# A two-block transformer kernel: the calls of the first attention, of the gated delta rule and of the start of the last attention in another order

## The chip, the cores and the metric

The kernel runs on one core of one Trainium2 chip. The metric is the device time of one launch in microseconds (us); the median over runs is compared. The five engines are called PE (TensorE, matmuls), DVE (VectorE), ACT (ScalarE), POOL (GpSimd) and SP (SyncE, which issues the DMAs).

## The reference, cut to what matters

256 tokens of width 1024 go through two blocks. The first has two layers, each an attention and an MLP; the second has a gated delta rule layer (GDN) and a last attention (FoX) on shared keys and values.

```python
def mla_mixer(h, ...):                       # first attention, 8 heads
    proj = h @ w_in                          # 384 q rank, 256 kv rank, 64 rope
    q  = (rms_norm(c_q,  g) @ w_uq)          # 8 x (128 nope + 64 rope)
    kv = (rms_norm(c_kv, g) @ w_ukv)         # 8 x (128 k + 128 v)
    q_pe = rope(rms_norm(q_pe, g), cos, sin)
    ...                                      # softmax(q k^T + q_pe k_pe^T) v, then w_o

def gdn_mixer(h, ...):
    qkv, z, a, b = split(h @ w_in)
    qkv = silu(causal_depthwise_conv(qkv, conv_w))
    ...                                      # g = log decay, beta
    a_mat = where(strict, (k*beta) @ k^T * decay, 0)    # 64 x 64, a chunk and a head
    sol = triangular_solve(a_mat, [v*beta, k*beta*exp(gcum)], unit_diagonal=True)
    ...                                      # 4 chunks in turn
    o = rms_norm_2(o, o_norm) * silu(z)
    return o @ w_out

def second_block(x, ...):
    h = x + rms_norm_2(gdn_mixer(...), g)
    k, v, c = shared_kv(h, ...)              # c: cumulated forget gate
    return h + rms_norm_2(fox_mixer(h, k, v, c, ...), g)
```

## The kernel before

Every engine has a program of its own inside `bass_two_blocks`: `tensor_program`, `scalar_program`, `vector_program`, `gpsimd_program`, `sync_program`. Each first defines small functions (one step each) and then calls them in a list **written out by hand**. An engine works its list strictly in order. Steps wait for each other by semaphores inside the functions, so the list sets what stands in front of what, and nothing else does. Nearly all instructions are recorded by a helper, so the profile shows one line each: PE's matmuls are L491 and its transposes L499, ACT's L1376 (table loads L1379), DVE's L2309, L2312 and L2315, POOL's L3525.

**Weights** come in 136 chunks through `RING` = 3 raw buffers: chunks 0 to 13 belong to the first attention (0 to 3 its first projection; kv, uq, uq, kv, uq, uq are 4 to 9; 10 to 13 the output weights), 14 to 45 to its MLP, 94 to 114 to GDN (109 and 110 the last of z, 111 to 114 the output weights), 115 to 135 to the last attention. float32 is split in two: `hi(c)` on ACT writes the high part `whi`, then `lo(c)` on DVE the rest `wlo` = `raw` - `whi`. For the chunks 104, 106, ..., 114 (`ON_POOL`) POOL does `lo(c)`, in four instructions. `hi(c)` waits until PE has finished chunk c-3. On PE a chunk is four quarters; `to(n, q)` works off the quarters up to, not including, quarter q of chunk n. A uq chunk issues something only in its quarters 1 and 3. Activations are split alike (`xhl`, in the last part of the inverse used again; `oth` and `otl`).

**First attention.** `turn_x` transposes the input, chunks 0 to 3 give the projection in four PSUM banks; `proj_scale` (half on ACT, half on DVE) reads them, `turn_c(0..4)` transposes the result, chunks 4 to 9 follow. `bias_mm` builds the relative bias of the second attention from indicator rows that DVE makes (`bias_ind`, 1.22 us each). For each of four head pairs i POOL rotates q (`q_rope(i)`: one multiplication and 12 small instructions, all on POOL), `qp_T(i)` transposes what it made, then `score_pair`, softmax on DVE and ACT (`logits`, `exp`, `over_sum`, `divide`), `turn_p`, `value`.

**GDN.** `sums(h)`, `rw_T`, `row_bc(h)`, `kq(h)` and DVE's `block_(h)` build for each of 8 heads the triangular matrix. The inverse is made for four groups of two heads, g = 0..3, in two pairs. `inv_0`, `inv_c`, `inv_r` and DVE's `inv_d`, `inv_b` (13 small dependent instructions), `inv_e` make the 8 x 8 diagonal blocks. Then come the levels l = 3..6: PE's `inv_w(g,l)` (product), ACT's copy, PE's `inv_x(g,l)` (product), DVE's addition, PE's `inv_v(g,l)` (transpose), ACT's copy; POOL masks one operand of each level. Then `inv_f`, `inv_t`, `inv_y` and `sol(h, part)`, the solution. `conv_pre`, `conv_taps`, `conv_acc` and `v_silu` are the convolutions and their silu, `v_T` turns v, `z_silu(pair, t)` is the silu of z. Groups 0 and 1 run at 696 to 717 us, groups 2 and 3 from 719 us on.

**Start of the last attention.** `turn_xf` transposes the sum of the residual; `xhi_kv` and `xlo_kv` split it; chunk 116 on needs them.

Of the kernel before, what the change touches and what calls it, by code (L numbers as in the profile page):

```python
# [132 lines left out]
def bass_two_blocks(nc, A, out):  # L133

    ctx = ExitStack()
    with ctx:
# [335 lines left out]
        def tensor_program(eng):  # L472
# [35 lines left out]
            def quarter(c, q):  # L508
# [3 lines left out]
                if q == 0:  # L512
                    L.wait_ge(*LO[c])
# [636 lines left out]
            to(104, 3)  # L1150
            sums(5)
            to(105, 3)
            sums(6)
            to(106, 1)
            sums(7)
            to(106, 3)
            rw_T()
            to(107, 0)
            row_bc(0)
            row_bc(1)  # L1160
            kq(0)
            to(107, 1)
            row_bc(2)
            to(107, 2)
            row_bc(3)
            kq(1)
            to(108, 1)
            kq(2)
            row_bc(4)
            to(108, 2)  # L1170
            kq(3)
            row_bc(5)
            to(109, 0)
            kq(4)
            kq(5)
            to(109, 1)
            row_bc(6)
            row_bc(7)
            kq(6)
            to(109, 2)  # L1180
            kq(7)
            inv_c(0)
# [18 lines left out]
            inv_x(1, 4)  # L1201
            inv_x(0, 4)
# [2701 lines left out]
```

## Time and profile before

| | us |
|---|---|
| median of 3 runs (lowest, highest) | 922.52 (921.96, 923.47) |
| span of the profiled execution | 920.4 |
| PE busy | 892.8 (97%) |
| DVE, ACT, POOL busy | 623.8, 525.5, 78.3 |
| DMA, mean rate | 155 GB/s |

The profile is of one execution. PE is busy nearly all the time and makes up 88% of the chain that ended last, so read it by PE's gaps: in which stretch PE is not busy, and what it waits for there.

### The profile page before, as it was taken

Reading aid. Unit: us, or ns where it says so; the run is one execution under the profiler, and the core shown is the slowest. Engines: PE = TensorE matmul, PEld = TensorE weight load, DVE = VectorE, ACT = ScalarE, POOL = GpSimd, SP = SyncE. Lnnn points to the kernel's source line nnn. Section 1 sums busy time; section 2 is a strip of 40 time slices with the busy share of each in tenths; the row PEclk is TensorE's granted clock in tenths of the full one; section 3 lists DMA queues with packets and bytes.
Section 4 is the critical chain, followed back from the end, with each engine's and each line's share of the span. In section 5 each row is a group of like instructions: output and inputs, shape, how many; then the busy total and the mean of one; then the engine's idle time right before and its main releaser. Section 6 shows DMA issues by size and latency. Waiting matters only on the chain.

```text
span 920.4 us, 13095 instructions
## 1 busy us (share of the span) xinstructions
PE 892.8 (97%) x5254; PEld 774.4 (84%) x5254; DVE 623.8 (68%) x1033; ACT 525.5 (57%) x848; POOL 78.3 (9%) x96
## 2 busy tenths in 40 slices
PE   6899999999999999999999999999999999999997
PEld 6777888888888888888888888999988888798885
DVE  6887686756666576657655556696786666776775
ACT  5788644435444686636444434565546565657782
POOL 0055000000000000000000000002535312000000
PEclk9999999999999999999999999999999799999999
DMA  8442456535554544447555654555430041654411
GB/s 261 138 150 81 138 183 245 187 137 184 201 195 153 183 137 141 150 153 242 179 189 175 222 197 139 182 160 166 138 101 37 5 157 46 203 190 180 165 65 46
DMA packets 61677, 142.67 MB, mean 155 GB/s; under 512 B 5296, under 2 KB 7344, under 8 KB 61616
## 3 DMA queue, kind: packets, MB, share of 16 engines
q1 hardware_dynamic: 61616, 141.83, 45.3%
q8 instruction: 42, 0.69, 0.3%
q14 instruction: 19, 0.16, 0.1%
HBM read 140.77 MB, written 1.05 MB: 154 GB/s over the span
## 4 chain that ended last, share of the span: by engine, by line
PE 88%; DVE 4%; POOL 3%; issue 2%; ACT 1%; SPq 1%; DMA 0%; DVEq 0%; POOLq 0%; ACTq 0%
PE ps L491 85%; PE ps L499 4%; POOL arena L3525 3%; SPq L3617 1%; DVE wlo L2309 1%; DVE sub L2309 1%; ACT arena L1376 0%; ACT whi L1376 0%; DVE xhl L2309 0%; POOL otl L3525 0%; DMA pint<-rel_bias_table_dram 0%; DVE arena L2309 0%; DVE X L2309 0%; DVE arena L2315 0%; ACT otl L1376 0%
## 5 line engine op out<-in xcount | busy, mean ns | idle before, releaser
L2309 DVE TENSOR_TENSOR wlo<-raw,whi 128x2048 fp32r<-128x2048 f32 (+3 forms) x130 | 286.8, 2214 | 121.7 <-ACT whi L1376 121.5
L1376 ACT ACTIVATE whi<-raw 128x2048 fp32r<-128x2048 f32 (+3 forms) x136 | 250.8, 1852 | 178.7 <-PE ps L491 166.7
L491 PE MATMUL ps<-xhl,whi 128*128 128x512 f32 (+3 forms) x928 | 257.7, 348 | 0.0
L491 PE MATMUL ps<-xhl,wlo 128*128 128x256 f32 x720 | 202.5, 281 | 0.0
L491 PEld LDWEIGHTS ps<-xhl,whi 128*128 128x128 f32 (+2 forms) x928 | 158.9, 186 | 25.0
L491 PE MATMUL ps<-whi,xhl 128*128 128x512 f32 (+2 forms) x528 | 168.9, 388 | 1.9 <-DVE xhl L2315 1.7
L491 PE MATMUL ps<-whi,oth 128*128 128x512 f32 x416 | 164.8, 396 | 0.2 <-DVE otl L2315 0.2
L491 PE MATMUL ps<-whi,otl 128*128 128x512 f32 x416 | 162.4, 390 | 0.0
L491 PE MATMUL ps<-wlo,oth 128*128 128x512 f32 x416 | 162.1, 390 | 0.0
L491 PEld LDWEIGHTS ps<-xhl,wlo 128*128 128x128 f32 x720 | 134.9, 187 | 0.8
L491 PEld LDWEIGHTS ps<-whi,xhl 128*128 128x128 f32 x528 | 99.2, 190 | 18.9 <-DVE wlo L2309 3.2
L491 PE MATMUL ps<-wlo,xhl 128*128 128x512 f32 (+2 forms) x264 | 100.1, 379 | 0.0
L1376 ACT ACTIVATE arena<-ps 128x256 f32<-128x256 f32 (+3 forms) x136 | 51.5, 417 | 77.2 <-PE ps L491 68.8
L491 PEld LDWEIGHTS ps<-whi,otl 128*128 128x128 f32 x416 | 78.1, 188 | 16.8
L491 PEld LDWEIGHTS ps<-whi,oth 128*128 128x128 f32 x416 | 78.1, 188 | 16.3 <-issue 0.7
L491 PEld LDWEIGHTS ps<-wlo,oth 128*128 128x128 f32 x416 | 78.2, 188 | 15.0
L3525 POOL TENSOR_TENSOR wlo<-raw,whi 128x512 fp32r<-128x512 f32 x24 | 35.0, 1488 | 600.4 <-ACT whi L1376 600.4
L2309 DVE TENSOR_TENSOR arena<-ps,arena 128x256 f32<-128x256 f32 (+2 forms) x104 | 45.7, 470 | 40.5 <-ACT arena L1376 20.3
L491 PE MATMUL ps<-arena 128*128 128x128 f32 (+3 forms) x384 | 65.9, 324 | 0.3
L1376 ACT ACTIVATE arena<-ps,st 128x512 f32<-128x512 f32 (+3 forms) x66 | 40.5, 639 | 41.0 <-PE ps L491 16.0
L491 PEld LDWEIGHTS ps<-arena 128*128 128x128 f32 (+1 forms) x384 | 55.7, 195 | 6.8 <-issue 1.7
L491 PEld LDWEIGHTS ps<-wlo,xhl 128*128 128x128 f32 x264 | 50.3, 191 | 7.1
(146 smaller groups left out, 880.9 us busy)
## 6 DMA issues: line engine op xcount, KB each, us to landing
raw<-mlp_w_in_dram SPq DMA_DIRECT2D x32, 1024.0 KB, 5.2
raw<-mlp_w_out_dram SPq DMA_DIRECT2D x32, 1024.0 KB, 5.0
raw<-gdn_w_in_dram SPq DMA_DIRECT2D x16, 1024.0 KB, 5.3
raw<-moba_w_qkv_dram SPq DMA_DIRECT2D x12, 1024.0 KB, 5.2
raw<-kv_w_dram SPq DMA_DIRECT2D x8, 1024.0 KB, 5.4
raw<-fox_w_in_dram SPq DMA_DIRECT2D x8, 1024.0 KB, 5.2
raw<-mla_w_o_dram SPq DMA_DIRECT2D x4, 1024.0 KB, 5.4
raw<-moba_w_o_dram SPq DMA_DIRECT2D x4, 1024.0 KB, 5.9
```

Source lines behind the costliest of these rows:

```text
L491: return eng.matmul(o, l, r, start=start, stop=True, skip_group_check=True)
L499: return eng.transpose(o, i, ident)
L1376: return eng.activation(o, i, f, **kw)
L2309: return eng.tensor_tensor(o, a, b, f)
L3525: return eng.tensor_tensor(o, a, b, f)
L3617: eng.dma_start(o, i).then_inc(s_in, 16)
```

## The change

The change gives the lists of PE, ACT and DVE the same calls as before, in another order, in three regions; POOL's and SP's lists stay word for word. Nothing of the computation changes. One condition is new: a uq chunk waits for its `lo` in quarter 1 and not in quarter 0, which issues nothing.

Cut to its core (`...` is left out; in GDN, `kq`, `row_bc` and `sums` move ahead of several quarters in the same manner):

```diff
-                if q == 0:
+                if q == (1 if kind == "uq" else 0):
                     L.wait_ge(*LO[c])
...
# tensor_program, first attention
+            to(0, 2)
             turn_x("mla", 3)
-            to(1, 3)
+            to(4, 0)
             bias_mm(0)
-            to(4, 0)
             turn_c(0)
...
             score_pair(0)
-            to(8, 2)
+            to(9, 2)
             qp_T(1)
-            to(9, 2)
             turn_p("mla", 0)
+            turn_p("mla", 1)
             score_pair(1)
-            turn_p("mla", 1)
...
-            to(10, 3)
+            to(11, 0)
             q_T(2)
             qp_T(2)
-            to(11, 0)
+            q_T(3)
             turn_p("mla", 2)
-            q_T(3)
+            turn_p("mla", 3)
             score_pair(2)
-            turn_p("mla", 3)
             qp_T(3)
...
# tensor_program, GDN
             to(109, 0)
-            kq(4)
-            kq(5)
+            inv_0(0)
             to(109, 1)
...
-            to(109, 3)
-            inv_r(0)
-            to(110, 1)
-            v_T(0, 0)
-            inv_0(0)
-            v_T(0, 1)
             inv_0(1)
             inv_w(0, 3)
-            v_T(1, 0)
+            kq(7)
             inv_w(1, 3)
+            to(109, 2)
+            v_T(0, 0)
             inv_x(0, 3)
             inv_x(1, 3)
-            v_T(1, 1)
-            inv_v(0, 3)
+            to(109, 3)
             inv_v(1, 3)
             inv_w(1, 4)
+            inv_v(0, 3)
             inv_w(0, 4)
+            to(110, 1)
+            inv_x(0, 4)
+            inv_x(1, 4)
             to(110, 2)
...
             inv_y(0)
-            inv_t(1)
             inv_r(1)
             sol(0, 0)
+            inv_t(1)
...
             inv_x(3, 5)
-            to(111, 1)
             inv_x(2, 6)
             inv_v(3, 5)
             inv_w(3, 6)
+            to(111, 1)
+            inv_x(3, 6)
...
# scalar_program, first attention
             rsq("mla_x")
-            hi(4)
+            proj_scale()
             hi(5)
-            hi(6)
-            proj_scale()
...
# scalar_program, GDN
             ln_sums()
+            conv_acc(8)
+            hi(106)
+            hi(107)
...
             inv_w(1, 3)
+            hi(111)
+            inv_y(1, 3)
             inv_y(0, 3)
-            z_silu(0, 0)
-            inv_y(1, 3)
+            inv_w(0, 4)
+            conv_acc(11)
             inv_w(1, 4)
-            z_silu(0, 1)
-            inv_w(0, 4)
-            z_silu(1, 0)
+            hi(112)
+            v_silu(1)
             inv_y(1, 4)
...
             inv_t(0)
-            hi(113)
+            z_silu(1, 0)
             z_silu(1, 1)
+            inv_t(1)
+            sol(0, 0)
             table("natural_log_exp_and_others")
-            inv_t(1)
...
             sol(2, 0)
+            hi(113)
# vector_program, first attention
             bias_table()
-            bias_ind(0)
             lo(2)
...
# vector_program, GDN
             inv_x(0, 3)
             inv_x(1, 3)
-            v_beta(1, 1)
-            lo(111)
+            conv_taps(10)
+            conv_taps(11)
             inv_x(1, 4)
             inv_x(0, 4)
...
# tensor_program, start of the last attention
             turn_xf(0, 1)
-            to(115, 0)
+            to(114, 3)
             turn_xf(0, 2)
```

**ACT at the projection's scaling**, before. `arena<-ps,st 128x352` are `proj_scale`'s two halves, `whi<-raw` a chunk's `hi` (here 4, 5 and 6):

```order
19 L1376 ACTIVATE st<-st 128x2 [waits s_rm]
20 L1376 ACTIVATE st<-st 128x2 [waits o_act]
21 L1376 ACTIVATE whi<-raw 128x2048 [waits s_w,s_raw1]
22 L1376 ACTIVATE whi<-raw 128x1152 [waits s_w,s_raw2]
23 L1376 ACTIVATE whi<-raw 128x1152 [waits s_w,s_raw0]
24 L1376 ACTIVATE arena<-ps,st 128x352 [waits s_rs]
25 L1376 ACTIVATE arena<-ps,st 128x352
```

The same place of the change:

```order
20 L1372 ACTIVATE st<-st 128x2 [waits s_rm]
21 L1372 ACTIVATE st<-st 128x2 [waits o_act]
22 L1372 ACTIVATE arena<-ps,st 128x352 [waits s_w,s_rs]
23 L1372 ACTIVATE arena<-ps,st 128x352
24 L1372 ACTIVATE whi<-raw 128x1152 [waits s_raw2]
25 L1372 ACTIVATE xhl<-ps,cols 128x256 [waits s_pt_] x3
```

The scaling now stands ahead of `hi(5)` and `hi(6)`; `hi(4)` went further ahead.

**PE in level 3 of groups 0 and 1**, before. `ps<-cst` are transposes, `oth,otl` and `otl,oth` the level's products (`inv_w`, `inv_x`), `ps<-cst,arena` here `v_T`:

```order
3114 L491 MATMUL ps<-oth,otl 128x128 [waits g_v,g_il0,g_ia0]
3115 L491 MATMUL ps<-oth,otl 128x128 x3
3116 L499 MATMUL ps<-cst,arena 128x128 [waits g_sv]
3117 L499 MATMUL ps<-cst,arena 128x128 x3
3118 L491 MATMUL ps<-oth,otl 128x128 [waits g_v,g_il1,g_ia1]
3119 L491 MATMUL ps<-oth,otl 128x128 x3
3120 L491 MATMUL ps<-otl,oth 128x128 [waits g_ia0]
3121 L491 MATMUL ps<-otl,oth 128x128 x3
3122 L491 MATMUL ps<-otl,oth 128x128 [waits g_ia1]
3123 L491 MATMUL ps<-otl,oth 128x128 x3
```

The same place of the change; `whi,xhl` and `wlo,xhl 128x512` are a quarter of chunk 109, `ps<-arena` are `kq(7)`:

```order
3091 L491 MATMUL ps<-oth,otl 128x128 [waits g_il1,g_ia1]
3092 L491 MATMUL ps<-oth,otl 128x128 x3
3093 L491 MATMUL ps<-whi,xhl 128x512
3094 L491 MATMUL ps<-wlo,xhl 128x512
3095 L491 MATMUL ps<-whi,xhl 128x512 x2
3096 L491 MATMUL ps<-wlo,xhl 128x512
3097 L491 MATMUL ps<-whi,xhl 128x512
3098 L499 MATMUL ps<-cst,arena 128x128 [waits g_ia0,g_sv]
3099 L499 MATMUL ps<-cst,arena 128x128 x3
3100 L491 MATMUL ps<-otl,oth 128x128 [waits g_ba]
3101 L491 MATMUL ps<-otl,oth 128x128 x3
```

A quarter now stands between `inv_w(1,3)` and `inv_x(0,3)`, whose input ACT copies meanwhile.

**ACT where pair 1 begins**, before. `oth<-ps` with g_ip0 is `inv_t(0)`, with g_ip1 `inv_t(1)`; `whi<-raw` is `hi(113)`:

```order
508 L1376 ACTIVATE oth<-ps 128x512 [waits g_ip0]
509 L1376 ACTIVATE whi<-raw 128x2048 [waits s_w,s_raw2]
510 L1376 ACTIVATE arena<-ps,st 128x512
511 L1379 ACT_TABLE_LOAD
512 L1376 ACTIVATE oth<-ps 128x512 [waits g_ip1]
```

The same place of the change:

```order
507 L1372 ACTIVATE oth<-ps 128x512 [waits g_ip0]
508 L1372 ACTIVATE arena<-ps,st 128x512 [waits s_w] x2
509 L1372 ACTIVATE oth<-ps 128x512 [waits g_ip1]
510 L1372 ACTIVATE arena<-ps 128x128 [waits g_sp0]
511 L1375 ACT_TABLE_LOAD
```

`inv_t(1)` no longer stands behind `hi(113)` and the table load, but behind two `z_silu`.

## Rows read from the trace of the kernel before

**Rows 1.** The page: busy time of the engines, and the chain by engine
```profile
PE 892.8 (97%) x5254; PEld 774.4 (84%) x5254; DVE 623.8 (68%) x1033; ACT 525.5 (57%) x848; POOL 78.3 (9%) x96
PE 88%; DVE 4%; POOL 3%; issue 2%; ACT 1%; SPq 1%; DMA 0%; DVEq 0%; POOLq 0%; ACTq 0%
```
**Rows 2.** Windows: length, busy us (count) of each engine, granted clock, DMA share, GB/s
```profile
600.00:630.00 30.00, 30.00 (x252) 30.00 (x253) 28.05 (x49) 18.13 (x25) 0.00 (x0) 1.00 0.54 176
690.00:700.00 10.00, 9.41 (x63) 8.22 (x62) 7.33 (x24) 7.81 (x9) 2.37 (x3) 1.00 0.24 93
700.00:710.00 10.00, 9.12 (x67) 7.95 (x67) 6.55 (x9) 6.44 (x12) 7.85 (x7) 1.00 0.00 0
720.00:730.00 10.00, 8.13 (x37) 7.41 (x38) 5.19 (x18) 5.05 (x10) 2.50 (x3) 0.61 0.00 0
730.00:740.00 10.00, 9.93 (x78) 9.72 (x78) 6.50 (x14) 6.50 (x17) 3.68 (x4) 0.88 0.46 157
```
**Rows 3.** PE's waits at 0 to 112 us: total, times, longest
```profile
PE ps L499 <- DMA X<-x_dram: 7.7, 1, 7.7
PE ps L499 <- POOL arena L3525: 3.4, 4, 1.5
PE ps L499 <- ACT arena L1376: 2.2, 1, 2.2
```
**Rows 4.** Timeline, 28 to 33 us: start, duration, engine, instruction, [idle before <-releaser]
```profile
28.69 1.16 ACT L1376 ACTIVATE whi<-raw 128x1152 fp32r<-128x1152 f32 x1 [1.30 <-PE ps L491]
28.71 1.08 DVE L2312 TENSOR_SCALAR arena<-ps,st 128x352 f32<-128x352 f32 x2 [1.79 <-PE ps L491]
29.76 0.98 ACT L1376 ACTIVATE arena<-ps,st 128x352 f32<-128x352 f32 x2
30.80 1.10 PE L499 MATMUL ps<-cst,arena 128*128 128x128 f32 x8 [2.20 <-ACT arena L1376]
32.92 0.76 PE L491 MATMUL ps<-whi,xhl 128*128 128x512 f32 x1 [1.03 <-DVE xhl L2315]
```
**Rows 5.** Timelines of PE and POOL, 60 to 85 us: q's rotation and who waits
```profile
60.48 0.33 PE L491 MATMUL ps<-wlo,xhl 128*128 128x384 f32 x1
60.65 0.34 PE L491 MATMUL ps<-whi,xhl 128*128 128x384 f32 x1
62.33 0.44 PE L499 MATMUL ps<-cst,arena 128*128 128x128 f32 x2 [1.34 <-POOL arena L3525]
72.06 0.99 POOL L3525 TENSOR_TENSOR arena<-arena,st 128x256 f32<-128x256 f32 x1 [9.79 <-DVE st L2315]
84.52 0.44 PE L499 MATMUL ps<-cst,arena 128*128 128x128 f32 x2 [1.52 <-POOL arena L3525]
```
**Rows 6.** POOL's timeline: `lo` of chunks 104 and 110
```profile
631.13 5.04 POOL L3525 TENSOR_TENSOR wlo<-raw,whi 128x512 fp32r<-128x512 f32 x4 [546.67 <-ACT whi L1376]
681.00 7.08 POOL L3525 TENSOR_TENSOR wlo<-raw,whi 128x512 fp32r<-128x512 f32 x4 [14.00 <-ACT whi L1376]
```
**Rows 7.** PE's waits at 690 to 750 us, and one of 750 to 810
```profile
PE ps L491 <- ACT oth L1376: 1.4, 1, 1.4
PE ps L499 <- DVE oth L2309: 0.6, 1, 0.6
PE ps L491 <- ACT otl L1376: 0.5, 2, 0.3
...
PE ps L491 <- DVE xhl L2315: 0.7, 1, 0.7
```
**Rows 8.** Timeline, 717 to 724 us: start of pair 1
```profile
717.41 1.91 ACT L1376 ACTIVATE whi<-raw 128x2048 fp32r<-128x2048 f32 x1
719.91 1.28 ACT L1379 ACT_TABLE_LOAD   x1
722.95 1.29 DVE L2309 TENSOR_TENSOR xhl<-sub,blk 128x512 fp32r<-128x512 f32 x2
723.70 1.97 PE L499 MATMUL ps<-cst,xhl 128*128 128x128 f32 x8 [0.51 <-DVE xhl L2309]
```

More of the change, by code:

```diff
@@ L1154, in tensor_program @@
+            to(105, 0)
+            rw_T()
+            to(105, 1)
+            row_bc(0)
+            to(105, 2)
+            row_bc(1)
             to(106, 1)
-            sums(7)
+            kq(0)
+            kq(1)
+            row_bc(2)
+            row_bc(3)
             to(106, 3)
[L1157 to L1166, printed above, removed]
+            kq(2)
@@ L1167, in tensor_program @@
+            kq(3)
+            row_bc(4)
+            row_bc(5)
+            to(108, 0)
+            kq(4)
             to(108, 1)
-            kq(2)
-            row_bc(4)
+            row_bc(6)
+            inv_c(0)
+            kq(5)
+            row_bc(7)
             to(108, 2)
-            kq(3)
-            row_bc(5)
+            inv_r(0)
+            kq(6)
             to(109, 0)
-            kq(4)
-            kq(5)
+            inv_0(0)
             to(109, 1)
-            row_bc(6)
-            row_bc(7)
@@ L1197, in tensor_program @@
             inv_v(1, 3)
             inv_w(1, 4)
+            inv_v(0, 3)
             inv_w(0, 4)
+            to(110, 1)
+            inv_x(0, 4)
+            inv_x(1, 4)
             to(110, 2)
-            inv_x(1, 4)
-            inv_x(0, 4)
+            v_T(0, 1)
             inv_v(1, 4)
             inv_w(1, 5)
+            v_T(1, 0)
             inv_v(0, 4)
+            v_T(1, 1)
             inv_w(0, 5)
@@ L2131, in scalar_program @@
             inv_w(0, 5)
+            z_silu(0, 1)
             inv_y(1, 5)
@@ L2136, in scalar_program @@
             inv_t(0)
-            hi(113)
+            z_silu(1, 0)
             z_silu(1, 1)
+            inv_t(1)
+            sol(0, 0)
             table("natural_log_exp_and_others")
-            inv_t(1)
+            inv_0(3)
             sol(1, 0)
-            sol(0, 0)
-            inv_0(3)
             inv_0(2)
@@ L2148, in scalar_program @@
             sol(2, 0)
+            hi(113)
+            sol(0, 2)
             sol(1, 2)
@@ L2948, in vector_program @@
             xlo("mla", 1)
-            gain("mla")
             xlo("mla", 2)
+            lo(1)
             xlo("mla", 3)
-            lo(1)
             read_positions()
             bias_table()
-            bias_ind(0)
             lo(2)
-            mean_x("mla")
             rope_angle()
             lo(3)
-            bias_ind(1)
+            mean_x("mla")
+            bias_ind(0)
+            lo(4)
+            rsq_b("mla_x")
             rope_cos()
-            rsq_b("mla_x")
+            proj_scale()
             rope_table()
-            proj_scale()
-            lo(4)
             c_lo(0)
+            gain("mla")
             c_lo(1)
+            lo(5)
             c_lo(2)
-            bias_add(0)
-            lo(5)
+            lo(6)
+            c_lo(3)
             c_mean()
-            c_lo(3)
             c_lo(4)
             rsq_b("mla_c")
+            k_rope()
+            bias_add(0)
+            bias_ind(1)
             bias_ind(2)
-            k_rope()
-            lo(6)
             k_sums(0)
@@ L2995, in vector_program @@
             over_sum("mla", 0)
+            over_sum("mla", 1)
             k_sums(1)
-            over_sum("mla", 1)
             lo(10)
+            q_sums(2)
+            logits("mla", 2)
             rsq_b("mla_k1")
-            logits("mla", 2)
-            q_sums(2)
             o_lo("mla", 0)
@@ L3315, in vector_program @@
             decay_arg(3)
-            conv_taps(11)
+            conv_pre(9)
+            conv_pre(10)
+            inv_0(0)
             block_(2)
+            block_(3)
             decay_arg(4)
-            inv_0(0)
-            block_(3)
+            inv_0(1)
+            conv_taps(9)
+            conv_pre(11)
             decay_arg(5)
@@ L3323, in vector_program @@
             block_(4)
+            decay_arg(6)
+            inv_d(0)
             block_(5)
-            decay_arg(6)
             decay_arg(7)
-            inv_0(1)
-            block_(6)
-            block_(7)
-            inv_d(0)
             inv_b(0)
@@ L3363, in vector_program @@
             inv_x(2, 3)
+            sol(2)
             lo(113)
-            sol(2)
             inv_x(2, 4)
@@ L3368, in vector_program @@
             inv_x(3, 4)
+            gain("fox")
             rsq_b("gdn_o0")
@@ L3385, in vector_program @@
             out_lo(1)
+            sol(6)
             sol(4)
             sol(7)
-            sol(6)
             sol(5)
@@ L3402, in vector_program @@
             post_add("gdn", 0, 0)
-            gain("fox")
             gained("gdn", 1)
             gained("gdn", 2)
+            post_add("gdn", 0, 1)
             xlo_kv(0, 0)
             xlo_kv(0, 1)
-            post_add("gdn", 0, 1)
             lo(116)
```

282 lines of the change are left out of this document (134 added, 148 removed).

## The prediction

> **What bounds the kernel now.** First the page's busy times and its chain: PE is busy for 892.8 of 920.4 us and makes up 88% of the chain [rows 1]. So a change of order can win only in PE's gaps, 27.6 us in all. Second, the busy time by windows, to see where the gaps lie. Between the regions of the change PE leaves nothing (30.00 of 30.00 us at 600 to 630) [rows 2]; gaps stand at the start, in the first attention, and from 690 to 750 us. Third, PE's waits in those regions. In the first attention 7.7 us are the load of the input before anything can run, and stay. What an order can touch is 3.4 us in four waits for POOL and 2.2 us in one wait for ACT [rows 3]. In GDN it is one wait of 1.4 us for ACT, 0.6 and 0.5 us, and some of 0.2 to 0.3 [rows 7]; the windows 690 to 710 leave 0.59 + 0.88 = 1.47 us of PE idle [rows 2]. Fourth, the clock: the granted clock is 0.61 and 0.88 in the windows 720 to 730 and 730 to 740 [rows 2], so PE ran at 1.2 instead of 2.4 GHz for 2 x (0.39 + 0.12) x 10 = 10.2 us there.
>
> A wait costs more than its bracket says, because the busy time of a matmul overlaps the next one. The last two matmuls before the wait at 62.33 start at 60.48 and 60.65, 0.17 us apart; the next starts 1.68 us later, where the bracket says 1.34 [rows 5]. So each wait counts its bracket and about 0.17 us more.
>
> **First attention, the projection.** Before, chunk 3 is done at about 28.6, then ACT does a `hi` of 1.16 us (28.69) and only then its half of the scaling, 29.76 to 30.74; DVE's half runs 28.71 to 29.79, and the transposes of `turn_c` start at 30.80 [rows 4]. In the change ACT scales first, and its half reads the two banks that are done first, so DVE's half is last: `turn_c` could start at 29.85, which is 0.95 us earlier. On top, `bias_mm(0)` and the `bias_ind(0)` that it waits for no longer stand ahead of chunk 2 and of `lo(2)`. The matmuls of `bias_mm(0)`, 0.6 us, move into the gap before `turn_c`, where PE is idle. I take 0.75 us for that; its bounds are 0 (if `lo(2)` ends as late as before) and 1.2 us (the matmuls and the 0.6 us that PE waits before them). Sum 1.7 us at `turn_c`. The wait of 1.03 us for `c_lo` at 32.92 [rows 4] stays, since ACT and DVE still split what PE has just transposed; I take 1.5 us at chunk 4.
>
> **First attention, the rotations.** POOL's rotations are released by DVE, and PE meets four waits for it, the longest 1.52 us at 84.52 and 1.34 us at 62.33 [rows 3, 5]. The gain at chunk 4 and an earlier `rsq_b` on DVE carry to the first of them: I take 2.1 us, and `qp_T(0)` comes 2.1 us earlier with its wait about as before, because the rotation sets it. `qp_T(1)` was one unit of a uq chunk after `score_pair(0)` and is now three after. A unit is nine matmuls at 0.17 us, 1.6 us [rows 5]; two more are 3.1 us, and the wait of 1.34 is less: it goes, 1.5 us. What is late next is DVE: `turn_p(0)` and `turn_p(1)` come in a row, for 0.3 to 0.4 us. The third rotation sat idle 9.79 us until DVE released it at 72.06, and the wait at 84.52 is for the fourth [rows 5]. The two run back to back, 12.4 us together, so PE's arrival is limited by DVE's release at 72.06, not by PE: PE comes 3.3 us earlier but leaves `qp_T(3)` only as much earlier as the release moves. `q_sums(2)` and `rsq_b("mla_q2")` follow the earlier uq chunks and stand before one `logits` as before: about 2.5 us. So of the gains so far 2.5 us leave the stretch, and PE waits about 2.5 us more than now for POOL. After it, `turn_p(4)` and `turn_p(5)` follow `score_pair(3)` with no quarter between, and cost about 0.5 us. **Attention: 2.0 us, bounds 0.5 and 3.3** (nothing of the release's move; all of it and no new waits).
>
> **GDN, pair 0.** The changed PE list puts a quarter (six matmuls of 512 columns; by the 0.17 us of 384 columns [rows 5], 1.4 us) between `inv_w` and `inv_x` of level 3, and quarters or `v_T` into level 4, where before a level's steps followed each other directly. The waits there are 0.6 (DVE), 0.5 in two (ACT), 0.2 (POOL) and two of 0.2 [rows 7]: with 0.17 each some 2.5 us, and a quarter covers any of them. These quarters are not new work, they are taken from ahead of the inverse. So 2.5 us is the upper bound of this term. Against it stand new tight places. (1) `hi(106)` now comes after `ln_sums` on ACT, and POOL needs 5.04 to 7.08 us for a `lo` [rows 6]: chunk 106 may be late by 0 to 1.1 us. (2) `row_bc(4)`, `lo(108)` and `inv_0(0)` come sooner after what they need from DVE and POOL, 0.1 to 0.5 us each. (3) POOL's mask for level 3 stands behind `lo(110)`, which took 7.08 us where DVE was at work beside it: 0 to 0.8 us. (4) `conv_taps(10)`, `conv_taps(11)` on DVE and `conv_acc(11)`, `hi(112)` (1.9 us, as `hi(113)` in [rows 8]) and `v_silu(1)` on ACT now stand inside the levels, ahead of steps that PE waits for; levels 4 and 5 have quarters only in part: 0.5 to 0.85 us. I take 0.1 + 0.3 + 0.2 + 0.5 = 1.1 us. **Net 1.4 us, bounds 0 and 2.5.** The move of the uq wait costs and gives nothing here, since in GDN there is no uq chunk; in the attention it lets PE pass into chunks that issue nothing, 0 to 0.3 us, counted above.
>
> The Trainium skill ("GPSIMD Engine Reference", Specifications) says that GpSimd shares its SBUF interfaces with VectorE and contends with VectorE instructions of two SBUF inputs. The trace agrees in direction: four instructions took 5.04 us at 631 and 7.08 us at 681 [rows 6]. That speaks against this change, which moves `conv_taps` and `lo(109)` about; it changes only the odds of places (1) and (3).
>
> **GDN, pair 1.** Before, `inv_t(1)` on ACT stands behind `hi(113)` (717.41, 1.91 us), one `z_silu` and a table load (719.91, 1.28 us), and PE waits 1.4 us for it [rows 7, 8]. Now only two `z_silu` of 0.7 us stand ahead. ACT is free 2.5 us sooner. But the next thing PE needs is `inv_0(3)`, which waits for DVE's `inv_d`, `inv_b`, `inv_e`; the last of it starts at 722.95 and PE goes on at 723.70 [rows 8]. DVE's chain there begins with the same inputs and has the same 16 instructions, one after the other. So the wait mostly moves from ACT to DVE and is not removed: 0.3 us, bounds 0 and 1.5. The clock falls at 722 in this very gap [rows 2], and since about 1.5 us of waiting stays in it, I leave the 10.2 us at half rate as they are. One `to(111, 1)` moves between `inv_w(3,6)` and `inv_x(3,6)` and the other quarters between `sol` steps: 0.1 us, bounds -0.3 and 0.4. `sol(0,0)` ahead of the table load on ACT: nothing, it is covered by the DVE chain.
>
> **Start of the last attention.** `turn_xf(0, 2)` comes two quarters earlier and `few_T`, `across`, `c_mm` later. The one wait here, 0.7 us for DVE's `xlo_kv` before chunk 116 [rows 7], hangs on `hi(116)`, `post_square` and `lo(116)` in a row, none of which moves ahead. DVE's `lo(119)` and `lo(120)` ahead of `xlo("fox")` have quarters of chunks 117 and 118 as cover. 0 us, bounds -0.3 and 0.3.
>
> **Sum.** 2.0 + 1.4 + 0.3 + 0.1 + 0 = 3.8 us; since small waits turn up where several steps become tight together, I take 3.5 us. The profiled span is 920.4 and the median 922.52, 2.1 us more outside it. 920.4 - 3.5 + 2.1 = 919.0 us.
>
> **Rivals.** (a) *The clock stays up.* If the gap at 719 to 724 becomes short enough, or later, that the clock doesn't fall, PE gets back up to half of the 10.2 us, less what waits take anyway: 4.5 us more, 914.5 us. For it: the wait for ACT goes. Against it: DVE's chain remains. The attention's short fall of the clock (the 512-column matmul at 32.92 took 0.76 us [rows 4]) is worth at most 1.7 us, and lies in the bounds above. The Trainium skill ("TensorE: Matmul & The Clock Gate", Part 4) says that transposes don't count as PE being busy in the same way. By that rule the levels, a third of them transposes, would draw the clock down as soon as quarters no longer separate them; in the window 700 to 710 they are mixed and the clock is 1.00 [rows 2], so the trace doesn't bear it out, and the change mixes more.
> (b) *The waits form again.* ACT's and DVE's own chains through the levels, and POOL, bound them, whatever PE does between: then the change doesn't do in GDN what it says, the 1.4 us are 0, and the attention gives its lower half, 1.0. 920.4 - 1.0 + 2.1 = 921.5 us. For it: PE was 97% busy, and ACT was not idle (7.81 and 6.44 of 10) [rows 2].
> (c) *Slower.* `hi(111)`, `hi(112)` and `v_silu(1)` on ACT, 4.5 us with 0.7 for the silu, stand in levels 3 to 5 ahead of copies that PE needs. If PE has then less than their length of other work left, it waits 1.9 us or more in one piece, as at 720, and the clock falls there as it fell at 722: another 10 us at half rate, 4.5 us. -3.5 + 1.9 + 4.5 = 2.9 us: 925.4 us. It decides from a gap of about 1.9 us in the levels; before, the longest there is 0.6 [rows 7].
>
> **Chances.** The forecast's case (917 to 920.7): 0.58. Rival (a): 0.12. Rival (b): 0.20. Rival (c): 0.10. The bounds of the terms are 0.5 + 0 + 0 - 0.3 - 0.3 = about 0 and 3.3 + 2.5 + 1.5 + 0.4 + 0.3 = 8.0 us; they will not all lie at one end. The range 914.6 to 922.8 takes in (a) and (b) and leaves out (c) and the tail. A measurement of this kernel can tell about 0.2%, 1.85 us, from no change: faster means below 920.7, slower above 924.4. That gives 0.70 faster, 0.20 the same, 0.10 slower.
>
> **What the profile would show.** Attention right: `turn_c` starts at 29 to 30, the wait before the second rotation's `qp_T` is gone, the one before the fourth is longer but ends near 82. GDN right: the window 690 to 710 leaves under 0.5 us of PE idle, and `inv_0(3)` starts about 3.4 us earlier than 723.70, its releaser still DVE. The clock at 0.5 for about 10 us after it. Wrong: a wait of over 1 us of PE for POOL at chunk 106 or level 3, or for ACT in levels 4 and 5; a clock under 1 before 715; or a gap at `turn_c` as long as before, which would say that DVE, not ACT, had set it.

## The result: 22 us slower, and the profile after

The changed kernel takes 944.62 us (median of 4 runs, 941.39 to 945.32), the kernel before beside it 922.44. The ratio is 1.0238, 95% interval 1.0222 to 1.0253. The forecast was 919.0 us with a range up to 922.8: wrong in sign and far outside.

The page of the changed kernel: span, then busy time (share) and count by engine, then the chain that ended last. These answer to [rows 1].

```profile
span 939.6 us, 13097 instructions
PE 903.0 (96%) x5254; PEld 782.3 (83%) x5254; DVE 640.6 (68%) x1033; ACT 524.8 (56%) x848; POOL 77.3 (8%) x96
PE 83%; DVE 8%; POOL 3%; ACT 2%; issue 2%; SPq 1%; DMA 0%; DVEq 0%; ACTq 0%; POOLq 0%
```

Read three things from it. PE is idle for 939.6 - 903.0 = 36.6 us, before 27.6: 9.0 us more of waiting. PE is busy for 10.2 us more with the same 5254 matmuls: they took longer. And DVE is busy for 16.8 us more with the same 1033 instructions, which no part of the prediction had allowed for. Waiting and longer matmuls together are the 19.2 us between the two spans. The profiled run is the quickest of the four (941.39); its mean granted clock is 0.981, that of the others 0.972 to 0.974, before 0.991.

Windows of the changed kernel, columns as in [rows 2]: length, busy us (count) of PE, PEld, DVE, ACT, POOL, then the granted clock, DMA share and GB/s.

```profile
640.00:650.00 10.00, 7.67 (x56) 7.43 (x54) 7.54 (x19) 4.91 (x9) 0.00 (x0) 0.86 0.05 8
650.00:660.00 10.00, 10.00 (x58) 9.89 (x58) 2.25 (x12) 5.48 (x6) 4.68 (x4) 0.63 0.28 100
690.00:700.00 10.00, 6.31 (x30) 5.08 (x29) 9.02 (x18) 4.53 (x7) 7.22 (x6) 0.92 0.30 106
700.00:710.00 10.00, 10.00 (x63) 8.75 (x61) 4.48 (x11) 4.49 (x6) 2.29 (x2) 0.91 0.01 3
730.00:740.00 10.00, 8.88 (x44) 7.47 (x44) 6.33 (x20) 4.57 (x10) 2.46 (x3) 0.66 0.00 1
750.00:760.00 10.00, 8.41 (x40) 7.72 (x41) 8.00 (x21) 4.94 (x11) 1.31 (x1) 0.66 0.76 289
780.00:790.00 10.00, 7.04 (x26) 5.71 (x27) 6.32 (x8) 3.36 (x5) 1.97 (x2) 0.83 0.31 105
```

The stretch around 650, where PE left nothing before, now has a gap and half rate. At half rate PE ran for 2 x (1 - 0.981) x 939.6 = 36 us in all, before for 2 x (1 - 0.991) x 920.4 = 17 us.

PE's waits from 630 to 790 us in the changed kernel, the long ones (total, times, longest); before, those of [rows 7] were 1.4, 0.6, 0.5 and 0.7. The first row is two waits, 3.6 us in front of `out_T(3)` and 1.6 in front of `out_T(0)`; the others stand in front of `inv_0(0)`, `sums(4)`, `inv_c(1)` and `kq(5)`:

```profile
PE ps L499 <- DVE arena L2311: 5.1, 2, 3.6
PE ps L499 <- DVE oth L2305: 3.7, 1, 3.7
PE ps L491 <- DVE st L2308: 2.3, 1, 2.3
PE ps L491 <- DVE xhl L2305: 1.1, 1, 1.1
PE ps L491 <- DVE arena L2311: 1.0, 1, 1.0
```

Comparing the start of the same quarter of the same chunk in both traces shows where the time goes, since the quarters come in the same order in both. (Inside GDN such a difference also holds the calls that the change moved across the quarter; at its end it doesn't.) Chunk 14, the first MLP: 109.27 against 111.67, 2.4 us **earlier**, and still 2.4 us at chunk 94. Chunk 111: 758.29 against 743.44, 14.9 us later. Chunk 113: 785.73 against 767.29, 18.4 later. Chunk 115: 19.3, and 19.25 at chunk 132. So the attention won, GDN lost 21.7 us, and the start of the last attention did nothing.

The 21.7 us add up. PE's waits in GDN sum to about 15 us, before to about 4: 11 us more. The windows from 640 to 790 us hold 31 us at half rate, before 10 us, and half of the difference, 10 us, is lost. Of the 11 us, 8.1 stand at three places, `inv_0(0)` (3.7 after 0.6), `out_T(0)` (1.6 after 0.2) and `out_T(3)` (3.6 after none); 2.3 stand at `sums(4)`.

### The profile page after: what moved, and what is told of

The parts are those of the page before. It is cut to its first block, busy times and chain, and to the rows that moved or that the text cites. A ratio compares the mean times of both kernels' runs of the same rounds, so it can differ in the third digit from the quotient of the medians.

```text
span 939.6 us, 13097 instructions
## 1 busy us (share of the span) xinstructions
PE 903.0 (96%) x5254; PEld 782.3 (83%) x5254; DVE 640.6 (68%) x1033; ACT 524.8 (56%) x848; POOL 77.3 (8%) x96
## 4 chain that ended last, share of the span: by engine, by line
PE 83%; DVE 8%; POOL 3%; ACT 2%; issue 2%; SPq 1%; DMA 0%; DVEq 0%; ACTq 0%; POOLq 0%
PE ps L491 79%; PE ps L499 4%; POOL arena L3521 3%; DVE arena L2311 2%; DVE wlo L2305 1%; ACT arena L1372 1%; SPq L3613 1%; ACT whi L1372 1%; DVE arena L2305 1%; DVE sub L2305 1%; DMA raw<-mla_w_in_dram 0%; DVE st L2311 0%; DVE st L2305 0%; DVE otl L2305 0%; DVE xhl L2305 0%
## 5 line engine op out<-in xcount | busy, mean ns | idle before, releaser
L2305 DVE TENSOR_TENSOR wlo<-raw,whi 128x2048 fp32r<-128x2048 f32 (+3 forms) x130 | 287.7, 2221 | 129.9 <-ACT whi L1372 129.7
L2305 DVE TENSOR_TENSOR arena<-ps,arena 128x256 f32<-128x256 f32 (+2 forms) x104 | 45.3, 469 | 30.1 <-ACT arena L1372 19.4
```

The source lines that it names most:

```text
L2305: return eng.tensor_tensor(o, a, b, f)
```

## Where a DVE instruction gets five times as long

The longest waits are for DVE. Here is `inv_b(0)`, 13 small dependent instructions, in the kernel before (start, duration, engine, instruction):

```profile
694.02 0.20 DVE L2309 TENSOR_TENSOR sub<-ps,sub 128x40 f32<-128x40 f32 x1
694.26 0.20 DVE L2309 TENSOR_TENSOR sub<-sub 128x40 f32<-128x40 f32 x1
694.50 0.19 DVE L2309 TENSOR_TENSOR sub<-ps,sub 128x32 f32<-128x32 f32 x1
694.72 0.19 DVE L2309 TENSOR_TENSOR sub<-sub 128x32 f32<-128x32 f32 x1
```

and the same four in the changed kernel, with what POOL does meanwhile (`lo(110)`) and what PE meets at its end (`inv_0(0)`):

```profile
690.61 5.00 POOL L3521 TENSOR_TENSOR wlo<-raw,whi 128x512 fp32r<-128x512 f32 x4 [10.46 <-ACT whi L1372]
...
691.98 0.20 DVE L2305 TENSOR_TENSOR sub<-ps,sub 128x40 f32<-128x40 f32 x1
692.22 0.97 DVE L2305 TENSOR_TENSOR sub<-sub 128x40 f32<-128x40 f32 x1
693.22 0.19 DVE L2305 TENSOR_TENSOR sub<-ps,sub 128x32 f32<-128x32 f32 x1
693.44 0.99 DVE L2305 TENSOR_TENSOR sub<-sub 128x32 f32<-128x32 f32 x1
...
698.65 1.11 PE L499 MATMUL ps<-cst,oth 128*128 128x128 f32 x4 [3.69 <-DVE oth L2305]
```

Look at every second row. The subtraction whose one input is in PSUM (`ps`) takes 0.20 us in both. The product with both inputs in SBUF takes 0.20 alone and 0.97 beside POOL. POOL's four instructions, 5.00 us from 690.61 on, end at about 691.86, 693.11, 694.36 and 695.61; the DVE products end at 693.19, 694.43 and 695.65, each just behind one. (In the changed kernel the lines of the helpers are 4 lower: L2305 is L2309 of before.) In all, `inv_b(0)` takes 6.95 us instead of 2.97. In all fourteen traces of this study it is the same: where they meet POOL's instructions, DVE instructions with two SBUF inputs take up to 1.1 us longer, those with a PSUM input at most 0.02 us. By calls, the 16.8 us are 4.0 in `inv_b(0)`, 3.0 in `conv_taps(5)` (beside `lo(104)`), 2.9 in `rsq_b` of gdn_o3 (beside `lo(114)`), 2.1 in `conv_taps(9)` (beside `lo(108)`), 1.1 in `inv_0(3)`, 0.9 each in `gain("fox")` and `out_norm(0)` (both beside POOL's masks of level 6), `out_norm(3)` and `inv_0(1)`; `conv_taps(8)` takes 0.9 less. `lo(110)` slid from 681 [rows 6] to 690.6 because ACT's `hi(110)` was moved behind `decay(6)`.

The Trainium skill ("GPSIMD Engine Reference", Specifications) names contention of GpSimd with VectorE instructions of two SBUF inputs. The rows agree: 0.97 us beside POOL with two SBUF inputs, 0.20 with one in PSUM. The prediction cited it and gave it no price.

## The experiments

Theory P: the time in GDN is lost where DVE's short instructions with two SBUF inputs stand beside POOL. Besides it there are S, T and U on the sums (DVE's order; PE's list asking too early; ACT's order around `hi(106)`) and the rivals named with each run. Runs marked "one run" have no interval. The kernel before moved between 919.9 and 922.5 from one set of runs to the next, and the four runs of the changed kernel differ by 3.9 us, so a difference of two single runs is read by its trace: between which chunks it arises, and whether the edit stands there.

### Only the attention: a gain

Kernel before, with the change's attention lists and the new place of the uq wait, nothing else.

> Only the first attention's new order (PE, ACT and DVE) and the new place of the uq wait, everything from the first MLP on as before. In the changed kernel's trace the first MLP's first quarter starts 2.4 us earlier than before (109.27 against 111.67) and the lead stays at 2.40 until chunk 94. Theory 'the attention is a gain, the loss is all in GDN': 920.0 us, 2.4 less than before (ratio 0.9974). Rival 'the lead is lost again when GDN's waits for DMA or DVE stay at their place': 922.4, no difference.

Measured: 918.9 us (10 runs) against 921.93 (13 runs), ratio 0.9972, interval 0.9961 to 0.9983. PE's waits for POOL in the attention are two instead of four:

```profile
PE ps L499 <- DMA X<-x_dram: 7.6, 1, 7.6
PE ps L499 <- POOL arena L3522: 2.9, 2, 2.1
PE ps L491 <- DVE wlo L2306: 1.4, 1, 1.4
```

The gain is real, and stands to the end: 3.1 us at chunk 14 in this trace, 3.8 at chunk 132. In the changed kernel, whose attention is the same, it is 2.4 at chunk 14. Both wait 2.1 us in front of `qp_T(3)`, at 81 us; behind it the clock falls in the changed kernel and stays up here (windows of the changed kernel, then of this one):

```profile
80.00:90.00 10.00, 9.40 (x46) 7.62 (x47) 4.41 (x14) 7.76 (x23) 0.54 (x2) 0.83 0.14 55
80.00:90.00 10.00, 8.54 (x49) 6.81 (x50) 5.04 (x16) 8.21 (x25) 1.18 (x5) 1.00 0.22 85
```

This is the fastest kernel of the study.

### One swap in the kernel before costs 7 us

```diff
             rsq("gdn_o2")
+            hi(114)
             rsq("gdn_o3")
-            hi(114)
```

> The kernel before with that one swap made: hi(114) ahead of rsq(gdn_o3) on ACT. Nothing else differs. hi(114) can't start before 761.2 us, since it waits for chunk 111 on PE. Theory P: rsq_b(gdn_o3) takes about 3.5 us instead of 0.56 beside lo(114), out_T(3) starts about 4 us later than 764.11, the kernel takes 4 us longer, 926.5. Rival Q: rsq(gdn_o3) ends at 763.6, DVE needs 0.6 and 1.1 us more, out_T(3) starts at 765.5, the kernel takes 1.3 us longer, 923.7.

Measured: 929.45 us (one run), 7.5 over the kernel before; PE goes from chunk 112 to chunk 113 in 13.4 us instead of 6.3, so 7.1 arise at the swap. POOL's `lo(114)` and `rsq_b`'s three instructions:

```profile
763.44 4.93 POOL L3525 TENSOR_TENSOR wlo<-raw,whi 128x512 fp32r<-128x512 f32 x4 [20.98 <-ACT whi L1376]
...
763.72 1.01 DVE L2315 SCALAR_TENSOR_TENSOR st<-st 128x4 f32<-128x4 f32 x1 [2.64 <-ACT st L1376]
764.77 1.18 DVE L2309 TENSOR_TENSOR st<-st 128x4 f32<-128x4 f32 x1
765.99 1.19 DVE L2315 SCALAR_TENSOR_TENSOR st<-st 128x4 f32<-128x4 f32 x1
```

Four numbers a partition, and 1.2 us each. PE waits 5.3 us in front of `out_T(2)`, where it waited not at all, and the clock is at half for 3.4 us from there on. Rival Q, order alone, allowed 1.3 us: out. P expected 4; the rest fits the list, since the kernel before has both `rsq_b` ahead of both `out_norm`, so `out_T(2)` is late too.

### The same swap, POOL's instructions half as long

```diff
-                n = CHUNKS[c]["a"] * CHUNKS[c]["b"] // 4
-                for i in range(4):
+                m = 8 if c == 114 else 4
+                n = CHUNKS[c]["a"] * CHUNKS[c]["b"] // m
+                for i in range(m):
```

> As the previous one (the kernel before, hi(114) ahead of rsq(gdn_o3)), and POOL makes lo(114) in eight instructions of 256 columns instead of four of 512. Theory P, with the stop lasting until the end of POOL's instruction under way: the three small instructions of rsq_b take about half, 1.8 to 2.1 us instead of 3.5, and out_T(3) comes 1.5 to 2 us earlier than in the previous kernel. Rival P2 (DVE and POOL share bandwidth, whatever the length of the instructions): rsq_b as long as in the previous kernel, no gain. Rival Q: the same as the previous kernel, 1.3 us over the kernel before.

Measured: 928.19 us (one run). The three instructions:

```profile
762.11 0.47 DVE L2315 SCALAR_TENSOR_TENSOR st<-st 128x4 f32<-128x4 f32 x1 [2.66 <-ACT st L1376]
762.62 0.65 DVE L2309 TENSOR_TENSOR st<-st 128x4 f32<-128x4 f32 x1
763.29 0.65 DVE L2315 SCALAR_TENSOR_TENSOR st<-st 128x4 f32<-128x4 f32 x1
```

1.83 instead of 3.46 us: the stand follows the length of POOL's instruction, as P says, and a share of bandwidth (P2) is out. But nothing was won with it. The wait in front of `out_T(2)` is 0.7 us shorter, one of 0.4 comes up in front of `out_T(3)`, and from chunk 112 to 113 PE takes 13.7 us after 13.4; the 1.3 us between the two runs stand already at chunk 112, ahead of the swap (1.6 there). P's 1.5 to 2 us at `out_T(3)` is missed. `lo(114)` takes 5.70 instead of 4.93 us and covers more of the eight instructions of `out_norm`, which took 4.60 instead of 3.27.

### The same split in the changed kernel

As above, for the chunks 110, 112 and 114; every order as in the change.

> The changed kernel, all orders as in the change, only that POOL makes lo(110), lo(112) and lo(114) in eight instructions of 256 columns each instead of four of 512. Theory P (a DVE instruction with both inputs in SBUF stands until POOL's instruction under way ends): the stand of each is halved; inv_b(0) takes about 5 instead of 6.95 us, rsq_b(gdn_o3) about 1.9 instead of 3.51, the waits before inv_0(0) and out_T(3) shrink from 3.9 and 3.7 to about 2.5 and 3 us: 2 to 3 us less, about 942 against the changed kernel's 944.6 (941.4 in its profiled run). Rival P2 (shared bandwidth): inv_b(0) and rsq_b as long as in the changed kernel, no gain. The lo itself takes 5.7 instead of 5.0 us.

Measured: 936.24 us (one run), 5.2 below the quickest and 8.4 below the median of the changed kernel. `inv_b(0)` takes 4.37 us, its products:

```profile
691.34 0.42 DVE L2305 TENSOR_TENSOR sub<-sub 128x40 f32<-128x40 f32 x1
...
692.02 0.43 DVE L2305 TENSOR_TENSOR sub<-sub 128x32 f32<-128x32 f32 x1
```

0.20 alone, 0.42 beside halves, 0.97 beside whole ones. PE's wait at `inv_0(0)` falls from 3.7 to 2.0 us, `rsq_b` of gdn_o3 takes 1.89 instead of 3.51, and the wait at `out_T(3)` falls from 3.6 to 2.8. P is shown in the changed kernel itself, without moving anything. Its share of the gain is smaller than the 5.2 us: 1.7 of them stand already at chunk 105, before the first split instruction runs, where both kernels wait the same 2.3 us and the half rate behind it is shorter here. The other 3.5 us are 2.0 of waits and less time at half rate.

### Undoing the swap in the changed kernel

```diff
             rsq("gdn_o2")
-            hi(114)
             rsq("gdn_o3")
+            hi(114)
```

> The changed kernel with one swap on ACT undone: rsq(gdn_o3) ahead of hi(114) again. In the changed kernel's trace three small DVE instructions (rsq_b of gdn_o3) take 3.51 us, before 0.56, while POOL works at lo(114), which hi(114) releases; PE then waits 3.6 us in front of out_T(3). Theory P (a DVE instruction stands still while POOL has an instruction under way, so the swap costs because it puts the two side by side): rsq_b takes 0.6 us again, the wait at out_T(3) is gone, 4 us or more less than the changed kernel, about 940.5. Rival Q (it is only that rsq(gdn_o3) comes 1.9 us later on ACT, behind hi(114)): about 2 us less, 942.5.

Measured: 937.21 us (one run), 4.2 below the changed kernel's profiled run and 7.4 below its median. `rsq_b` takes 0.56 us again. But the wait at `out_T(3)` is still 2.5 us, because `lo(114)` now meets `out_norm(3)`, whose four instructions take 4.20 instead of 1.13. That the time came out as P said is luck: 3.2 of the 4.2 us stand already at chunk 112, ahead of the swap, where the two kernels are the same. The swap is worth about 1 us here: the collision moved by one call. (In the kernel before it cost 7, because there it held up `out_T(2)` as well.)

### hi(110) earlier

On top of the previous kernel (the changed one with the swap undone):

```diff
             hi(109)
+            hi(110)
             decay(5)
             decay(6)
-            hi(110)
             decay(7)
```

> The changed kernel with rsq(gdn_o3) ahead of hi(114) again, and on ACT hi(110) moved back ahead of decay(5). In the changed kernel POOL's lo(110) runs 690.6 to 695.6 beside DVE's 13 small dependent instructions of inv_b(0), which take 6.95 us there and 2.97 before; PE then waits 3.7 us in front of inv_0(0). Theory P: hi(110) comes at about 682, lo(110) ends by 689, inv_b(0) takes 3.0 us again, the wait before inv_0(0) falls to under 0.5 us: 4 us less than with the first swap alone (937.2), 933.2. Rival R (the wait at inv_0(0) comes from the order of PE and DVE around row_bc(6), inv_c(0), inv_r(0)): the wait stays over 2.5 us, 936.5.

Measured: 937.39 us (one run): no gain, P's 933.2 missed. Yet its steps came true: `lo(110)` runs 682.0 to 689.0, `inv_b(0)` takes 3.73 us, the wait is down to 0.47, and PE goes from chunk 107 to chunk 109 in 694.23 - 674.27 = 20.0 us instead of 698.61 - 675.00 = 23.6. What became of it stands in the windows; first the previous kernel, then this one:

```profile
720.00:730.00 10.00, 8.60 (x57) 7.28 (x55) 9.87 (x11) 2.92 (x6) 8.11 (x5) 1.00 0.01 2
730.00:740.00 10.00, 9.05 (x41) 8.11 (x41) 5.19 (x19) 6.22 (x11) 2.44 (x3) 0.54 0.00 0
750.00:760.00 10.00, 8.08 (x64) 7.38 (x64) 9.56 (x21) 4.73 (x11) 1.30 (x1) 1.00 0.69 268
```
```profile
720.00:730.00 10.00, 7.79 (x44) 6.55 (x43) 9.04 (x22) 3.79 (x6) 4.23 (x4) 0.71 0.00 1
730.00:740.00 10.00, 10.00 (x57) 9.76 (x56) 3.71 (x9) 6.32 (x13) 2.28 (x2) 0.60 0.00 0
750.00:760.00 10.00, 10.00 (x50) 9.37 (x49) 6.25 (x14) 3.20 (x8) 0.00 (x0) 0.58 0.31 117
```

The wait of 1.6 us in front of `out_T(0)` is in both. In the one the clock stays at 1.00 after it, in the other it falls. A gain of some us ahead of such a gap can be given back by the clock behind it. Why it fell in one and not in the other stays open. By chunks, this kernel is 3.7 us ahead of the previous one at `inv_0(3)` and 0.4 behind it at chunk 112.

### The sums

On top of that: on DVE `sum_add(0)`, `(1)` ahead of `conv_taps(6)`, `sum_add(2)`, `(3)` ahead of `conv_taps(7)`.

> The previous kernel, and on DVE sum_add(0), (1) ahead of conv_taps(6) and sum_add(2), (3) ahead of conv_taps(7). In the changed kernel they stand behind both, and PE stands 2.33 us in front of sums(4), which needs the bank that sum_add(0) reads; the clock is 0.5 from there for about 10 us. Theory S (the order on DVE makes this wait): it is gone or under 0.7 us, 2 us less; if the clock then stays up, 5 to 6 us less. Rival T (PE's list asks for sums(4) to (7) before ACT has made their squares, conv_silu and qk_square in turn with conv_taps): the wait moves to sums(5) to (7), under 1 us less.

Measured: 932.01 us (one run), 5.4 less. PE's waits at 640 to 660 us:

```profile
PE ps L491 <- ACT arena L1372: 2.3, 2, 2.1
```

The wait of 2.3 us for DVE became one of 2.1 for ACT, one call later, in front of `sums(5)`: T is right on the wait, and its time (under 1 us less) is missed. The 5.4 us then come from elsewhere (less half rate at 720 to 760), so the run says nothing on the size of this step.

Neither S nor T asks why DVE is late at the sums, and the trace of the changed kernel has an answer:

```profile
630.18 5.42 DVE L2311 SCALAR_TENSOR_TENSOR arena<-arena,cols 128x255 f32<-128x255 f32 x6
639.42 2.45 DVE L2311 SCALAR_TENSOR_TENSOR arena<-arena,cols 128x255 f32<-128x255 f32 x6 [3.02 <-ACT arena L1372]
```

The first is `conv_taps(5)`, beside `lo(104)`: 5.42 us where `conv_taps(6)` in the second takes 2.45. ACT's `conv_silu(5)` waits for it, `hi(105)`, `conv_acc(6)`, `conv_taps(6)`, `(7)` and `sum_add(0)` follow in turn, and PE's wait for `sum_add(0)` is 2.3 us, less than the 3.0 that `conv_taps(5)` lost. So the wait at the sums may itself be a collision with POOL, at one remove. That is read off one chain and not tested: `conv_taps(5)` stands beside `lo(104)` in every run that has the changed order of the front of GDN.

On top again, on PE: `sums(5)`, `(6)`, `(7)`, `rw_T` and `row_bc(0)`, `(1)` one or two quarters later.

> The previous kernel, and PE's sums(5), (6), (7), rw_T and row_bc(0), (1) each one or two quarters later, so that a quarter stands between any two of sums(4) to (7). Theory T: the waits between sums(4) and chunk 104's quarter 2 are gone and the clock stays up at 646 to 657: 4 to 6 us less than the previous kernel. Theory S (all was DVE's order): less than 1 us less.

Measured: 936.24 us (one run), 4.2 more. PE's waits at 640 to 670 us:

```profile
PE ps L491 <- POOL wlo L3524: 4.8, 1, 4.8
PE ps L491 <- ACT arena L1375: 0.8, 2, 0.6
```

The waits for the sums are nearly gone, as T said, and 4.8 us for chunk 106 take their place; T's 4 to 6 us less are missed.

```diff
+            hi(106)
             table("natural_log_exp_and_others")
             ln_sums()
             conv_acc(8)
-            hi(106)
             hi(107)
```

> The kernel with the sums spread out (936.24), and on ACT hi(106) ahead of the table load and ln_sums, as before. With the sums spread, PE's waits at chunk 104 were gone, but 4.98 us came up in front of chunk 106, whose lo POOL makes in about 5 us after hi(106). Theory U (the changed order couples the two: hi(106) behind ln_sums forces all sums early, and either PE waits for the sums or for chunk 106): the 4.98 us go and the clock stays up there, 5 to 7 us less, 930. Rival (hi(106) isn't what POOL waits for): no change, 936.

Measured: 931.97 us (one run), 4.3 less. The wait for chunk 106 is gone, as U said: in the change `hi(106)` stands behind `ln_sums`, which needs all eight sums. But a new wait of 2.3 us for DVE stands in front of `rw_T`, and the kernel is no faster than the one before the sums were spread (932.01). That wait is P again: `decay_columns`, behind `ln_sums`, now runs beside `lo(106)` and takes 3.25 instead of 1.16 us, two of its eight instructions standing:

```profile
653.23 1.19 DVE L2314 SCALAR_TENSOR_TENSOR st<-st 128x16 f32<-128x16 f32 x1 [0.29 <-ACT st L1375]
654.34 0.17 DVE L2308 TENSOR_TENSOR st<-st 128x16 f32<-128x16 f32 x1
654.42 1.25 DVE L2314 SCALAR_TENSOR_TENSOR st<-st 128x16 f32<-128x16 f32 x1
```

### Only the front of GDN

The previous kernel, from `inv_t(0)` (ACT), `inv_x(0,5)` (PE), `inv_s(0)` (DVE) on as in the kernel before.

> The previous kernel, from inv_t(0) on ACT, inv_x(0,5) on PE and inv_s(0) on DVE on in the order of the kernel before: of GDN only the front with the inverse levels between quarters is changed. Theory P says that the rest of the loss sits in pair 1 and at out_T(0), out_T(3), where DVE's inv_0(3), gain, out_norm run beside POOL: 4 to 6 us less than the previous kernel, about 922 with the attention's gain of 2.6 in it. If the prediction's step on pair 0 holds (1.4 us for quarters between the levels), 918 or less, below the kernel with the new attention alone (918.9).

Measured: 926.47 us (one run), 5.5 less, within the 4 to 6 that P gave to pair 1 and what follows; the run shows where they were lost and not by what, since it puts back all of the order there. It is still 7.6 us over the new attention alone. In the levels the prediction's step holds; PE's waits at 693 to 715 us, one in place of the three (0.8 us) that the levels had before:

```profile
PE ps L491 <- ACT otl L1374: 0.2, 1, 0.2
```

The price stands ahead of them, at 640 to 692 us, where PE waited for nothing before:

```profile
PE ps L499 <- DVE st L2307: 2.3, 1, 2.3
PE ps L491 <- ACT arena L1374: 1.2, 3, 0.6
PE ps L491 <- DVE arena L2313: 1.0, 2, 0.8
PE ps L499 <- DVE oth L2307: 0.5, 1, 0.5
```

The last is `inv_0(0)`, 0.6 before. So there are 4.5 us of new waits to save 0.6. Of the first row, 2.3 us in front of `rw_T`, the two standing instructions of `decay_columns` beside `lo(106)` make 2.2.

### ACT out of the way of pair 1

Kernel before, ACT: `inv_t(0)`, `z_silu(1,1)`, `inv_t(1)`, table load; `hi(113)` behind `sol(2,0)`.

> The kernel before, only ACT's order where pair 1 begins: inv_t(0), z_silu(1,1), inv_t(1), then the table load, and hi(113) four calls later, behind sol(2,0). Before, PE waits 1.35 us for inv_t(1)'s copy and then 0.51 us for DVE's inv_e(3), and the clock falls at 722.2. The prediction's step: DVE's chain ends at 723.6 whatever ACT does, so the wait for ACT goes over to DVE, and inv_0(3) starts at most 0.3 us earlier than 723.70: 922. Rival: with ACT out of the way the waits shrink by over 1 us and the clock doesn't fall: 917.5.

Measured: 922.08 us (one run) beside 921.9 (one run). PE's waits at 715 to 726 us:

```profile
PE ps L499 <- DVE xhl L2309: 2.5, 1, 2.5
```

The waits of 1.4 for ACT and 0.5 for DVE [rows 7, 8] are one of 2.5 for DVE. The prediction's step on pair 1 is right: DVE's chain bounds this place.

### A smaller move in the same spirit

The new attention alone, and `inv_c(0)`, `inv_r(0)`, `inv_d(0)`, `inv_b(0)` about 2 us earlier, a quarter of chunk 110 behind `inv_0(1)`.

> The kernel with the new attention alone (918.9), and in GDN one small move: inv_c(0), inv_r(0) on PE and inv_d(0), inv_b(0) on DVE about 2 us earlier, with one quarter of chunk 110 between inv_0(1) and inv_w(0,3), so that the 0.59 us wait at inv_0(0) and the wait for the first copies go. POOL's masks of level 3 then start right behind lo(110), and partly beside inv_b(0). If the 13 instructions of inv_b(0) stay near 3 us: 1 to 1.5 us less, 917.6. If they run beside POOL they take up to 2 us more, and nothing is won: 919.

Measured: 919.9 us (9 runs), ratio to the kernel before 0.9978 (0.9968 to 0.9988), the attention alone 0.9972. Nothing won: the wait of 0.6 at `inv_0(0)` is gone, and PE stands 1.0 us in front of `inv_c(0)`, since DVE's `inv_0(1)` isn't ready that early. `inv_b(0)` took 2.98 us, so it met no POOL instruction, and by the expectation the time should have been 917.6: that is missed, for a reason it didn't name.

## Why the prediction was wrong, point by point

- **The attention: right in the sum, partly by luck.** 2.0 us were said, bounds 0.5 and 3.3; the runs of the attention alone give 2.6 by the ratio (0.28% of 922) and 3.0 by the medians, the trace of the changed kernel 2.4. `turn_c` starts at 29.53 (29 to 30 was said), the wait in front of the second `qp_T` is gone, the one before the fourth is 2.11 us and ends at 80.60, where 82 was said. So PE leaves the rotations 3.9 us earlier, where 2.5 was said, and PE waits 0.6 us more there, where about 2.5 was said: the release of the third rotation moved further than the working had it. Half rate behind this wait then took 1.5 us back, which the working had not, and the two errors cancelled.
- **Pair 0's levels: right in the levels, wrong in the sum.** The quarters do cover them. The step that failed is "Against it stand new tight places ... 1.1 us". It took 0.3, 0.2 and 0.5 us for the places (2), (3) and (4), and no DVE call in it was priced as standing beside POOL. Place (3) named `lo(110)`, but as something that POOL's mask would wait for; what stood beside it was `inv_b(0)`, 6.95 us instead of 2.97, and PE waited 3.7 us. The failing sentence is that the shared interface "changes only the odds": the trace of before had its price: `conv_taps(8)` beside `lo(106)` takes 3.3 us there, the other `conv_taps` alone 2.45. Over GDN the runs showed about 11 us of new waits, 8.1 of them at three places behind DVE calls that stood beside POOL, and about 10 us of half rate behind the waits, instead of 1.1 us in all.
- **The sums: left out.** The working took `sums`, `rw_T` and `row_bc` as free to move and priced only chunk 106, at 0 to 1.1 us. Their chain (squares on ACT, `conv_taps` on DVE, banks held by `sum_add`) waits 2.3 us and starts a stretch of half rate; how much of this is the order and how much `conv_taps(5)` beside `lo(104)` stays open.
- **Pair 1 and after.** The step on ACT was right (shown by the run with `hi(113)` late). "The other quarters between `sol` steps: 0.1 us" passed over the swap of `hi(114)` and `rsq("gdn_o3")` on ACT, two lines of the diff that the cut above leaves out, and over `gain("fox")`, moved beside POOL's mask: PE waits 3.6 and 1.6 us behind them, in front of `out_T(3)` and `out_T(0)`. Undoing the swap alone gave back only about 1 us, since `lo(114)` then met `out_norm(3)`.
- **The clock.** The sum left the 10.2 us at half rate as they were. In GDN they became 31.
- **The start of the last attention: right**, 0 us: 19.3 us later at chunk 115, 19.25 at chunk 132.
- **The rivals.** Rival (c) had half of the mechanism, a gap and then half rate, in the wrong place and once. Its gap was to come from ACT's `hi(111)`, `hi(112)` and `v_silu(1)` in the levels, and there PE waits 0.2 us for ACT. Gaps with half rate behind them came at 645, 695, 730, 750 and 780 us, for DVE. Of the signs of being wrong, "a clock under 1 before 715" came true; the waits that were named, for POOL and for ACT, did not. With 0.10 the slower case had too little chance, for a change that touches every call of a stretch where PE lost nothing.

## What to carry to other kernels

Before an instruction is moved in time, ask what runs on POOL beside its new place: short DVE instructions with two SBUF inputs, in a dependent chain, can each pay the rest of POOL's instruction under way. Here POOL instructions of half the length halved each stand, at the price of more POOL time: 3.5 us were won in the changed kernel, and nothing in the other one. Moving POOL's work (`hi(110)` earlier) freed one chain, and moving it by one call (`hi(114)`) only changed who stood beside it; so look at all the calls that the moved POOL work will cover. And a stretch in which the bound engine loses nothing has only downside: take the part of a reordering that touches a real gap (here the attention), and leave the rest.

A single run that lands on the expected time proves little when kernels of this kind differ by some us from run to run. Compare the traces chunk by chunk, and count only what arises where the edit stands.

## What the runs showed of the hardware

- A DVE instruction on 128x4 numbers with both inputs in SBUF took 0.16 us alone, 0.65 beside POOL instructions of about 0.7 us, 1.2 beside POOL instructions of about 1.25. With one input in PSUM there was no difference (128x40: 0.20 and 0.20).
- A DVE instruction with two SBUF inputs beside several POOL instructions in a row stood until the end of one of them and not of all: the products of `inv_b(0)` end within 0.1 us behind the ends of POOL's instructions, one behind each.
- Of equal waits, one was followed by a fall of the clock and one was not, at two places (1.6 us in front of `out_T(0)`, 2.1 us in front of `qp_T(3)`), so that single runs of nearly equal kernels differ by some us. The four runs of the changed kernel differ by 3.9 us, with mean clocks from 0.972 to 0.981.
